# Seven projections of the HGRN stage by seven products of quarters, with the weights' sums on GpSimd

## The reference

```python
def hgrn2_layer(h, w_in, b_in, lb, head_norm, w_out):       # h: 512 tokens x 1024
    proj = h @ w_in + b_in                                   # 1024 -> 4 x 1024
    fp, iv, qp, z = jnp.split(proj, 4, axis=-1)
    logf = jnp.log(lb + (1.0 - lb) * jax.nn.sigmoid(fp))
    k = (1.0 - lb) * jax.nn.sigmoid(-fp)
    q = jax.nn.silu(qp)
    o = hgrn2_chunkwise(heads(q, 8), heads(k, 8), heads(iv, 8), heads(logf, 8))
    o = rms_norm_2(o.transpose(0, 2, 1, 3), head_norm.reshape(8, 128)).reshape(b_, s_, 1024)
    return (o * jax.nn.silu(z)) @ w_out
...
def hgrn2_chunkwise(q, k, v, logf):
    """S_t = diag(f_t) S_{t-1} + k_t v_t^T (k_t = 1 - f_t); o_t = S_t^T q_t."""
```

## Time and profile before

| what | value |
|---|---|
| median of three runs | 1808.07 us (1807.0 to 1808.78) |
| profiled execution | 1809.41 us |
| its span | 1807.5 us, 19295 instructions |
| mean granted clock of TensorE | 0.980 |
| stage E | from 1434.65 us to the end |
| turns 1, 2, 3 begin at | 1492.60, 1563.69, 1635.36 us |
| tail begins at | 1707.02 us |

### The profile page before, as it was taken

One profiled execution on the slowest core, in us unless ns is written; L12 is line 12 of the kernel. 1 busy time (PEld: TensorE's weight loads), 2 busy tenths in 40 slices (PEclk: granted clock), 3 DMA queues, 4 the chain that ended last, 5 costly groups with the idle time before them and its releaser, 6 DMA issues.

```text
span 1807.5 us, 19295 instructions
## 1 busy us (share of the span) xinstructions
PE 1724.9 (95%) x7394; PEld 972.9 (54%) x7394; DVE 853.6 (47%) x1508; ACT 358.8 (20%) x650; POOL 209.3 (12%) x280
## 2 busy tenths in 40 slices
PE   6999999997899999999999999998899999999986
PEld 3878867675343433333344465677555544555543
DVE  3756633446232323233243357667656506446464
ACT  1122220001100000000022123300344315235220
POOL 1234300001000000000000000002245300000000
PEclk9999999998999999999999999999899999999998
DMA  6322122154799999999961223133200312111001
GB/s 274 111 91 85 47 105 85 61 233 186 304 407 426 426 427 426 425 427 428 422 279 59 70 94 117 53 110 108 93 1 1 117 47 94 47 47 47 1 0 47
DMA packets 27872, 308.60 MB, mean 171 GB/s; under 512 B 4415, under 2 KB 4703, under 8 KB 10368
## 3 DMA queue, kind: packets, MB, share of 16 engines
q1 hardware_dynamic: 21312, 289.21, 39.2%
q0 software_dynamic: 6464, 18.10, 2.9%
HBM read 306.57 MB, written 4.19 MB: 172 GB/s over the span
## 4 chain that ended last, share of the span: by engine, by line
PE 83%; DVE 11%; DMA 2%; issue 1%; ACT 1%; POOL 1%; DVEq 0%; POOLq 0%; SPq 0%; ACTq 0%
PE ps L408 78%; DVE arena L1161 6%; PE ps L411 5%; DMA wring<-in_w 2%; DVE arena L1172 1%; ACT arena L2239 1%; DVE arena L1188 1%; DVE small L1176 1%; POOL small L2626 1%; DVE H L1161 1%; DVE arena L1192 0%; DMA arena<-in_rows 0%; DVE arena L1257 0%; DVE HT L1188 0%; DVE wring L1161 0%
## 5 line engine op out<-in xcount | busy, mean ns | idle before, releaser
L408 PE MATMUL ps<-arena 128*64 128x512 f32 (+13 forms) x2384 | 534.2, 401 | 18.4 <-DVE arena L1172 8.4
L408 PE MATMUL ps<-wring,HT 128*128 128x512 f32 (+1 forms) x1216 | 476.9, 545 | 9.0 <-DVE HT L1188 6.3
L408 PEld LDWEIGHTS ps<-arena 128*64 128x64 f32 (+3 forms) x2384 | 244.4, 154 | 243.3 <-issue 227.6
L1161 DVE TENSOR_TENSOR arena<-ps,arena 128x512 f32<-128x512 f32 (+2 forms) x185 | 126.5, 684 | 520.1 <-PE ps L408 358.1
L408 PE MATMUL ps<-wring,arena 128*64 128x512 f32 (+2 forms) x1008 | 341.7, 580 | 4.3 <-DMA wring<-in_w 2.7
L408 PEld LDWEIGHTS ps<-wring,HT 128*128 128x128 f32 x1216 | 228.8, 193 | 216.5 <-issue 200.6
L2239 ACT ACTIVATE arena<-ps 128x512 f32<-128x512 f32 (+3 forms) x150 | 81.1, 540 | 584.6 <-PE ps L411 308.0
L408 PE MATMUL ps<-HT,wring 128*128 128x512 f32 (+2 forms) x528 | 193.3, 533 | 0.5 <-DVE arena L1188 0.5
L408 PEld LDWEIGHTS ps<-wring,arena 128*64 128x64 f32 (+1 forms) x1008 | 124.8, 150 | 97.4 <-issue 94.0
L2239 ACT ACTIVATE arena<-arena 128x512 f32<-128x512 f32 (+7 forms) x129 | 86.4, 670 | 450.6 <-DVE arena L1161 418.5
L1161 DVE TENSOR_TENSOR H<-ps,H 128x512 f32<-128x512 f32 x190 | 131.3, 691 | 92.3 <-PE ps L408 89.1
(11 more groups left out here) (106 smaller groups left out, 929.9 us busy)
## 6 DMA issues: line engine op xcount, KB each, us to landing
wring<-in_w SPq DMA_DIRECT2D x48, 2048.0 KB, 19.8
wring<-in_dense SPq DMA_DIRECT2D x39, 2048.0 KB, 8.2
arena<-in_w SPq DMA_DIRECT2D x36, 2048.0 KB, 18.8
HT<-in_w SPq DMA_DIRECT2D x12, 2048.0 KB, 16.9
arena<-in_rows POOLq DMA_DIRECT2D x33, 256.0 KB, 5.0
H<-in_x SPq DMA_DIRECT2D x4, 512.0 KB, 9.5
arena<-in_relb POOLq DMA_DIRECT2D x8, 256.0 KB, 8.3
n_scratch<-arena POOLq DMA_DIRECT2D x4, 512.0 KB, 3.3
```

Of the source, the lines that this page charges most:

```text
L408: return nc.tensor.matmul(o, l, r, start=start, stop=stop, skip_group_check=True)
L1161: done(nc.vector.tensor_tensor(o, a, b, op), tell)
```

## The change

Seven of the eight tiles of the stage, all but `o_y0`, are projected by seven products of quarters. In detail:

- The four sums of the rows are made once, by DVE, behind the last group of `o_y0`, in slot 0 of `wring`; the tiles then share slots 1 to 3.
- The weights' sums, four of 1024 elements a tile, are made by POOL (`sums_ahead`: T3, T2; `sums_behind`: T1, T4), which tells `sumg`.
- Gates and queries now arrive in quarters and are added up in SBUF: ACT copies bank a (`tooka`), DVE adds b and c. ACT's sigmoids of gates and queries follow when a tile is whole; the queries' multiplies on DVE come one tile later.
- Head 0's decay rows (`prep` parts 0 to 3) stand on DVE ahead of and behind the taking of product 1 of o_x, head 1's are spread over products 4 of o_x to 1 of o_y.
- Scores, states and outputs come behind products 3, 4, 5 of o_x (head 0) and 2, 3, 4 of o_y (head 1).
- POOL multiplies z by the norm's weights (`gain`, which tells `zn`), so that `pair_norm` has two multiplies; its reduction (`pair_squares`) ends the turn, and its multiplies come in the turn after.

```diff
-SLOT += [2, 0, 3, 1, 2, 0, 1, 0, 2, 1, 0, 2, 1, 0, 2, 1, 3, 0, 2, 1, 3, 0, 2, 1, 3]
+SLOT += [2, 0, 3, 1, 2, 0, 1, 0, 2, 1, 0, 2, 1, 0, 2, 1, 3, 2, 1, 3, 2, 1, 3, 2, 1]
...
+for _h in range(4):
+    SEVENS[f"o_x{_h}"] = (1, None)
+    if _h:
+        SEVENS[f"o_y{_h}"] = (0, None)
...
-GROUPS = [(4, 5, 6, 7, 0, 1, 2, 3)] + [tuple(range(8))] * 3
-
-
-PLAN = {2: (("scores", 0), ("prep", 1)), 3: (("states", 0),), 4: (("outs", 0),), 5: (("scores", 1),),
-        6: (("states", 1),), 7: (("outs", 1), ("norm", 0))}
+
+PLAN = {3: ("scores", 0), 4: ("states", 0), 5: ("outs", 0), 9: ("scores", 1), 10: ("states", 1), 11: ("outs", 1)}
...
+                        by = "sumg" if key[:2] == "o_" else "sumw"
+                        pe.wait_ge(S(by), saw(by))
...
+                    if was and key[:3] == "o_x" and bank == "a":
+                        pe.wait_ge(S("tooka"), saw("tooka"))
...
+                first_values()
                 for p in range(4):
-                    for n in GROUPS[p]:
-                        group(p, n)
-                        for what, c in PLAN.get(n, ()) if p else ():
-                            step(p - 1, what, c)
+                    for m in range(14 if p else 7):
+                        if m == 1 and not p:
+                            pe.wait_ge(S("suma"), 7)
+                        key = f"o_x{p}" if m < 7 else f"o_y{p}"
+                        for s in range(2):
+                            seventh(key, 2 * (m % 7) + s)
+                        if p and m in PLAN:
+                            step(p - 1, *PLAN[m])
...
+                def gates_queries(p, n):
+
+                    b, q, k = pB[p % 2], pQ[p % 2], f"o_x{p}"
+
+                    def half(x, i):
+                        return x[:, :, 256 * i:256 * i + 256]
+
+                    def bank(x):
+                        return F[k, x].ap.rearrange("p (s n) -> p s n", s=2)
+                    if n == 1:
+                        v.wait_ge(*past[k, n])
+                        v.wait_ge(S("tooka"), p + 1)
+                        tt(half(q, 0), bank("b"), half(q, 1), ADD, "took")
+                    elif n in (3, 4):
+                        v.wait_ge(*past[k, n])
+                        tt(half(q, 1), bank("b" if n == 3 else "c"), half(q, 1), ADD, "took")
+                    elif n == 5:
+                        f = full(k, "b")
+                        tt(half(b, 1), bank("b"), half(b, 1), ADD, f)
+                    elif n == 6:
+                        f = full(k, "c")
+                        tt(half(q, 0), bank("c"), half(q, 0), ADD, f)
...
-                    heard("hsq")
-                    red(ss, pB[p % 2].rearrange("p c n -> p (c n)").rearrange("p (x d) -> p x d", d=128), ADD, tell="hss")
                     heard("inv")
                     yx = yh.rearrange("p a (h d) -> p a h d", h=2)
                     tt(yx, yx, rr.rearrange("p (a h) -> p a h", a=4).unsqueeze(3).to_broadcast([128, 4, 2, 128]), MUL)
-                    v.wait_ge(S("hn"), 32)
-                    tt(yh, yh, hn[p // 2][:, 256 * (p % 2):256 * (p % 2) + 256].unsqueeze(1).to_broadcast([128, 4, 256]), MUL)
+                    v.wait_ge(S("zn"), p + 1)
...
+                for p in range(1, 4):
+                    y, r = f"o_y{p}", row("b_ivz" + "+" * p)
+                    prep(p - 1, 0, 0)
+                    prep(p - 1, 0, 1)
+                    gates_queries(p, 1)
+                    prep(p - 1, 0, 2)
+                    prep(p - 1, 0, 3)
+                    if p > 1:
+                        pair_norm(p - 2)
+                    gates_queries(p, 3)
+                    step(p - 1, "scores", 0)
+                    prep(p - 1, 1, 0)
+                    gates_queries(p, 4)
+                    gates_queries(p, 5)
+                    step(p - 1, "states", 0)
+                    prep(p - 1, 1, 1)
+                    gates_queries(p, 6)
+                    step(p - 1, "outs", 0)
+                    for n in range(7):
+                        seventh(y, n, behind(pvz[p % 2]), by_row(r))
+                        if n == 0:
+                            prep(p - 1, 1, 2)
+                        elif n == 1:
+                            prep(p - 1, 1, 3)
+                            queries(p)
+                        elif n == 2:
+                            row_done(r)
+                        elif n == 3:
+                            step(p - 1, "scores", 1)
+                        elif n == 4:
+                            step(p - 1, "states", 1)
+                        elif n == 5:
+                            step(p - 1, "outs", 1)
+                            z_half(p, 1)
+                    pair_squares(p - 1)
+                    z_half(p, 0)
                 for i in range(4):
                     y_turned(0, i, 0, 4)
-                prep(3, 0)
+                step(3, "prep", 0)
...
+                for p in range(1, 4):
+                    logs(p - 1, 0)
+                    gates_queries(p, 0)
+                    powers(p - 1, 0)
+                    gates_queries(p, 2)
+                    step(p - 1, "scores", 0)
+                    logs(p - 1, 1)
+                    powers(p - 1, 1)
+                    gates(p)
+                    queries(p)
+                    step(p - 1, "scores", 1)
+                    z_half(p, 1)
+                    pair_norm(p - 1)
+                    z_half(p, 0)
...
+            def sums_ahead(key, free):
+
+
+                w, (s, n, _) = of_weight(key), PLACE[key]
+                g.wait_ge(S(f"w{s}"), 16 * n)
+                sum_(w["T3"], w["B22"], w["B12"], SUB)
+                g.wait_ge(free.full, free.at)
+                sum_(w["T2"], w["T3"], w["B11"], ADD, "sumg")
+
+            def sums_behind(key):
+                w = of_weight(key)
+                g.wait_ge(*past[key, 0])
+                sum_(w["T1"], w["B22"], w["T2"], SUB, "sumg")
+                g.wait_ge(*past[key, 1])
+                sum_(w["T4"], w["B21"], w["T2"], SUB, "sumg")
+
+            def gain(p):
+
+                z = pvz[p % 2][:, :, 256:512]
+                g.wait_ge(S("hn"), 32)
+                g.wait_ge(S("zd"), p + 1)
+                nc.gpsimd.tensor_tensor(z, z, hn[p // 2][:, 256 * (p % 2):256 * (p % 2) + 256].unsqueeze(1).to_broadcast([128, 4, 256]),
+                                        MUL).then_inc(S("zn"), 1)
+            sums_ahead("o_x0", F["t", "E", 3, 1])
+            sums_behind("o_x0")
+            for p in range(1, 4):
+                sums_ahead(f"o_x{p}", F[f"o_y{p - 1}" if p > 1 else "o_x0", "b"])
+                if p > 1:
+                    head_roots(8)
+                sums_behind(f"o_x{p}")
+                gain(p - 1)
+                sums_ahead(f"o_y{p}", F[f"o_x{p}", "b"])
+                sums_behind(f"o_y{p}")
+            head_roots(8)
+            gain(3)
+            head_roots(8)
```

283 lines of the change are left out of this document (151 added, 132 removed).

## The result

The changed kernel took **1860.12 us** (median of 4 runs, 1858.33 to 1863.95) where the kernel before took 1808.41 (4 runs, 1807.0 to 1808.78): a ratio of 1.029, 95% interval 1.0272 to 1.0308. It is slower, as forecast, but by 52 us where 16 were forecast, and outside the range.

The account below looks back on a forecast made before the run. The prediction took TensorE, busy 95% of the span, as the bound. Terms without a clash gave -10.3 us, clashes +24.5 and clock behind waits +1.8: +16.0 on 1808.07, so 1824 us, range 1795 to 1836.

Parts of the forecast that it names:

- Seven projections, -23.6: On TensorE, seven projections by seven products each take 24.17 us instead of 27.54, a product 3.45: -23.6 us.
- Waits ahead of outputs, 2.05 each: Six outputs in the turns wait for VectorE to take a bank and make the states, 2.05 us each: +9.9 us.
- First scores at 16.1 us, second scores +1.0: Scores wait for VectorE's decay rows: first ones start 16.1 us into a turn (+6.4 us), second ones cost +3.0 in three turns.
- Start, +2.7: At the start, the four sums of the rows are ready 6.1 us after product 0 begins, which covers 3.45: +2.7 us.
- Tail, -6.5: Behind the turns, less norm work on VectorE shortens TensorE's waits, less 1.5 us more low clock: -6.5 us.
- POOL's instruction, 2.3 us, and early sums: GpSimd's additions and products of 1024 elements with two inputs take 2.3 us each, and every sum is early.
- The clash, 17 x 1.44 = +24.5: GpSimd's two-input instructions meet late VectorE rows 17 times, each costing VectorE 1.44 us by words read: +24.5 us.
- The clock, -2.2 and +1.8: Half the 1.5 us of low clock behind second scores goes in three turns (-2.2); TensorE's waits from clashes add +1.8.
- sum without clashes of 1797.8: All terms for the whole kernel without any clash between VectorE and GpSimd: -10.3 us.
- the first rival: GpSimd costs VectorE little, 0.36 us or less an instruction, served in its gaps: 1796 to 1804 us, chance 0.33.
- The rival with whole instructions held: Each clash costs VectorE the GpSimd instruction's whole 2.3 us: +31 us, 1839 us, chance 0.15.

Follow-up runs that it names:

- e8: e2 with the outputs one product later on TensorE, two products between states and outputs: 1809.07 us, ratio 1.0002 to the kernel before.
- e1: The changed kernel with GpSimd's sums and norm-weight product cut to 8 elements a partition instead of 1024, output wrong: 1817.73 us, ratio 1.0046 to the kernel before.
- e11: The changed kernel with GpSimd's sums replaced by a one-input multiply by 1 on 1024 elements, output wrong: 1838.21 us, ratio 1.0148 to the kernel before.
- e2: The changed kernel with two extra waits on GpSimd, so sums start behind the decay rows, norm-weight product last: 1822.77 us, ratio 1.0080 to the kernel before.
- e13: The kernel before plus four unread 128x1024 sums on GpSimd in each of turns 1 to 3, at the first decay rows: 1826.97 us, ratio 1.0095.
- e12: The changed kernel with each of GpSimd's sums made by four instructions of 256 elements: 1847.29 us, ratio 1.0205 to the kernel before.
- e15: The kernel before plus two unread 128x1024 additions on VectorE ahead of each chunk's last decay row in turns 1 to 3: 1826.23 us, ratio 1.0098.
- e9: e8 with the filler products of e7 ahead of a turn's first and second transposes: 1804.63 us, ratio .9977 to the kernel before.
- e16: e8 with first scores and first outputs one product later, T1, T4 and next T3 on VectorE, norm behind states: 1809.84 us, ratio 1.0000 to the kernel before.
- e7: e2 with unread filler products on TensorE, 3 ahead of a turn's first transposes and 1 ahead of its second: 1823.34 us, ratio 1.0081 to the kernel before.
- e14: e16 with one filler product of 128x256 ahead of each pair of transposes: 1808.36 us, ratio .9992 to the kernel before.

## Why the prediction was wrong, step by step

The direction was right; the size was wrong by 36 us, 30 or so of them in two terms of the sum, the clash and the clock.

- **Seven projections, -23.6**: right. Products start 3.45 us apart with no gap but where VectorE is late.
- **Waits ahead of outputs, 2.05 each**: right, 2.03 to 2.04 (one of the six 2.39); e8, in which they are gone, is 13.7 us faster.
- **First scores at 16.1 us, second scores +1.0**: right without a clash (16.0 and .84 in e1). With it they are 24.2 us and 5.64.
- **Start, +2.7**: the wait is right without a clash (2.47 in e1) and 4.49 with it. But the product behind it takes 5.41 us in e1 and 5.33 in the changed kernel instead of 3.62, and the sum had nothing for that.
- **Tail, -6.5**: got 3.0. The last wait is 6.77, 1.3 less as forecast, and the wait ahead of the outputs 2.81 (2.4 forecast). But the wait at the tail's start is 2.95 us where it was 1.36, which the step left out, and the outputs still run at low clock behind the shorter wait: 2.78 us where 1.80 was forecast.
- **POOL's instruction, 2.3 us, and early sums**: right, 2.35 us, and PE waited for no sum in the turns.
- **The clash, 17 x 1.44 = +24.5: the first step that failed.** "1.44 us if the loss goes by words" was scaled from one row of .36 us under a GpSimd instruction with *one* input. e11 shows that this is the cheap kind: .3 to .8 us even with 1024 elements. One with two inputs holds VectorE until it ends: 2.0 us where VectorE's own rows are short or of 1.2 us (the chain above, e2), 1.57 in e13. The changed kernel less e1 is 42.4 us (38.6 between the profiled executions), where this term and the clock's +1.8 had 26.3. Turn 2's first chain ended 8.2 us late and its second wait grew by 4.8: 13.0 for the 5.3 clashes counted, where 7.6 were forecast. The price explains 3.2 of these 5.4 us (5.3 clashes at 2.04 are 10.8); the count explains the rest, since all four instructions hit the first chain (3.7 counted) and the three of the second cost as much as 2.4 (1.6 counted). Over the stage the first chains are 7.7 to 8.2 us late, the second waits 4.8, 4.8 and 2.9 longer and the start's 2.0: 38 to 39 us, 19 clashes of 2.0 where 17 were counted. The Trainium skill (SBUF — State Buffer, Who interferes with whom) has the later instruction wait for the whole of the other. The chain above, and e12, where the copies wait for a piece, agree; the prediction had priced it as a rival at 1839 with a chance of .15. The same section of the Trainium skill says that it holds against a GpSimd instruction that reads SBUF; e11, where such reads with one input cost .3 to .8 of 2.8 us, differs, and the measurement decides.
- **The clock, -2.2 and +1.8: the second step that failed.** It should have been a cost of its own: 6.0 us a turn in e1 where .8 was left in the sum (15.6 us in three turns), and 8.2 in the changed kernel. The prediction treated PE's waits as costing their own length. The earlier trace rows already had a price: outputs at 3.32 us behind a wait of 6.06, which take 1.80 in the earlier trace rows. It was set aside as "mostly hidden". e15 shows that it isn't. How much of e1's 6.0 us is due to waits of .8 to 2.0 us, and how much to the scores in the new order, stays open: e9's filler took most of it away, and e16 has 3.2 us of it behind a wait of .3.

Together: e1 came 20 us above the sum without clashes of 1797.8, and the clash 16 above its term; 36 in all. In e1's profiled execution, 2 us further off, it is 16 by the clock in the turns, 4 by the tail and 2 at the start.

The direction is right in part for a reason that the prediction did not have. Its sum without a clash made the kernel 10.3 us faster; e1, without one, is still .46% slower than the kernel before, with 16 us of low clock in its turns that the sum did not have. So the first rival, faster by cheap clashes, fails even where there are none. The rival with whole instructions held had the mechanism of the clash, and its 1839 is 21 us short as well, with the same count and nearly the same clock term.

**What stays open.** What takes the clock where PE hardly waits. In e16's turn 1 PE waited .79 ahead of product 3, and the scores took 4.47 us and the product behind them 6.38; in turn 2 it waited 1.71, and they took 4.02 and 5.41; e7's runs spread over 12 us. In the rows read, waits of over 3 us ahead of scores were followed by low clock each time, shorter ones only sometimes, and second scores also with hardly any wait. Of e9's gain over e8 the filler is the cause, but e7 over e2 and e14 over e16 showed none that can be measured. Why a clash cost 1.57 in e13 and 2.0 elsewhere no run tells.

## What to carry to other kernels

- Before giving GpSimd an elementwise instruction with two inputs, look at what VectorE does in the next 2.35 us. If it is a chain that PE waits for, every such instruction costs that chain 1.6 to 2.0 us, however small the row that it meets; started behind the chain instead, by a wait on the semaphore that ends it, the same work cost at most 5 us in the whole kernel (e2 against e1) where it had cost 42.
- Add some 3 to 5 us for the clock to each long wait of PE, and not by its length: waits of 3.0 us (e15), 5.6 (changed kernel), 6.8 (e13) and 8.2 (changed kernel) were followed by 4.0, 4.8, 5.1 and 3.4 us of low clock.
- Where a step waits 2 us for VectorE, try one more product ahead of it: 13.7 us for moving six outputs by one product. Then look where the wait went; part of it stood ahead of product 3 of the next turn.
